# A fused three-branch token mixer on one core: attention steps moved in among the transposed products, and the gate path taken out of their evictions

## What is computed

```
h = RMSNorm(x)
(qa,ka,va,za, qb,ckv,iq,ik,iw,zb, qc,kc,vc,zc, ga,gb,gc) = split(h @ w_in)
ya = attention_A(qa, ka, va, sink, t5) * silu(za)     # 16 heads, window of 2 chunks of 64
yb = attention_B(qb, latent keys chosen by top-k 64 of an indexer) * silu(zb)
yc = attention_C(qc, kc, vc, relative bias) * silu(zc)
merged = sigmoid(ga)*(ya@w_pa) + sigmoid(gb)*(yb@w_pb) + sigmoid(gc)*(yc@w_pc)
out = RMSNorm(x + merged @ w_o)
```

## Time and profile before

| | |
|---|---|
| median of 3 runs | 973.84 us |
| the profiled execution | 973.51 us, of it 971.6 us span |
| TensorE busy | 961.6 us (99%) |
| weight loads of TensorE busy | 813.1 us (84%) |
| VectorE busy | 608.5 us (63%) |
| ScalarE busy | 473.0 us (49%) |
| GpSimd busy | 28.2 us (3%) |
| mean granted clock of TensorE | 0.997 |
| HBM | 195 GB/s over the span |

### The profile page before, as it was taken

One profiled execution on the slowest core, in us unless ns is written; L12 is line 12 of the kernel. 1 busy time (PEld: TensorE's weight loads), 2 busy tenths in 40 slices (PEclk: granted clock), 3 DMA queues, 4 the chain that ended last, 5 costly groups with the idle time before them and its releaser, 6 DMA issues.

```text
span 971.6 us, 13291 instructions
## 1 busy us (share of the span) xinstructions
PE 961.6 (99%) x5114; PEld 813.1 (84%) x5114; DVE 608.5 (63%) x1135; ACT 473.0 (49%) x786; POOL 28.2 (3%) x26
## 2 busy tenths in 40 slices
PE   9999999999999999999999999999999999999996
PEld 8788888888888888888888888888888888888885
DVE  7585755777675776586765655766655555555553
ACT  6564544555454545454453545544534443444442
POOL 0030000000000110010000000000000000000000
PEclk9999999999999999999999999999999999999998
DMA  8754755464653755564654745646555576555553
GB/s 342 274 194 130 244 200 187 151 225 162 207 205 120 253 174 180 189 207 157 222 199 139 261 157 178 227 149 216 167 193 179 191 304 221 186 184 187 174 177 126
DMA packets 54766, 190.34 MB, mean 196 GB/s; under 512 B 6192, under 2 KB 7088, under 8 KB 54064
## 3 DMA queue, kind: packets, MB, share of 16 engines
q1 hardware_dynamic: 54416, 189.23, 56.9%
q10 hardware_dynamic: 288, 0.27, 0.1%
HBM read 187.38 MB, written 2.10 MB: 195 GB/s over the span
## 4 chain that ended last, share of the span: by engine, by line
PE 94%; DVE 2%; DMA 2%; issue 1%; ACT 0%; SPq 0%; POOLq 0%; POOL 0%; DVEq 0%; ACTq 0%
PE bank L1025 23%; PE bank L1006 18%; PE bank L1008 18%; PE bank L1007 18%; PE bank L1028 12%; PE bank L981 2%; PE bank L1061 2%; PE bank L1081 2%; DMA raw<-in_w_s_dram 2%; DVE w_lo L626 1%; DVE hT L693 0%; ACT w_hi L444 0%; PE bank L1198 0%; DVE scores L686 0%; DVE denom L678 0%
## 5 line engine op out<-in xcount | busy, mean ns | idle before, releaser
L626 DVE TENSOR_TENSOR w_lo<-raw,w_hi 128x1024 fp32r<-128x1024 f32 (+2 forms) x326 | 387.2, 1211 | 172.8 <-ACT w_hi L444 171.4
L444 ACT ACTIVATE w_hi<-raw 128x1024 fp32r<-128x1024 f32 (+2 forms) x326 | 334.8, 1046 | 297.0 <-PE bank L1008 204.0
L1025 PE MATMUL bank<-hT,w_hi 128*128 128x512 f32 x976 | 306.2, 397 | 0.0
L1008 PE MATMUL bank<-w_hi,hT 128*128 128x512 f32 x568 | 221.1, 389 | 0.0
L1028 PEld LDWEIGHTS bank<-hT,w_lo 128*128 128x128 f32 x976 | 181.1, 188 | 41.1
L1006 PE MATMUL bank<-w_hi,hT 128*128 128x512 f32 x504 | 197.2, 391 | 0.0
L1007 PE MATMUL bank<-w_lo,hT 128*128 128x512 f32 x504 | 196.1, 389 | 0.0
L1028 PE MATMUL bank<-hT,w_lo 128*128 128x256 f32 x976 | 190.8, 278 | 0.0
L1025 PEld LDWEIGHTS bank<-hT,w_hi 128*128 128x128 f32 x976 | 150.6, 189 | 3.9
L1008 PEld LDWEIGHTS bank<-w_hi,hT 128*128 128x128 f32 x568 | 106.6, 188 | 22.3
L1006 PEld LDWEIGHTS bank<-w_hi,hT 128*128 128x128 f32 x504 | 94.6, 188 | 20.4 <-issue 0.2
(11 more groups left out here) (149 smaller groups left out, 559.6 us busy)
## 6 DMA issues: line engine op xcount, KB each, us to landing
raw<-in_w_s_dram SPq DMA_DIRECT2D x314, 512.0 KB, 4.4
bias_t<-in_bias_dram SPq DMA_DIRECT2D x24, 384.0 KB, 3.1
raw<-in_w_s_dram SPq DMA_DIRECT2D x6, 456.0 KB, 5.7
merged<-in_x_dram SPq DMA_DIRECT2D x2, 1024.0 KB, 10.5
raw<-in_w_s_dram SPq DMA_DIRECT2D x8, 256.0 KB, 3.1
big<-in_x_dram SPq DMA_DIRECT2D x1, 2048.0 KB, 9.8
out_dram<-big SPq DMA_DIRECT2D x8, 256.0 KB, 2.6
big<-in_x_t_dram SPq DMA_DIRECT2D x7, 256.0 KB, 5.9
```

The source lines that it names most:

```text
L444: nc.scalar.activation(halves(g)[0], raw[:, s, 0:n], ACT.Copy).then_inc(hi_ready, 1)
L626: nc.vector.tensor_tensor(low, raw[:, s, 0:n], high.bitcast(F32), ALU.subtract).then_inc(lo_ready, 1)
L1008: ins = mm(acc, xl, wh[:, e, :], start=False, stop=kt == n_kt - 1)
L1025: mm(bank[2 * (c % 2) + n][:, :], wh[:, e, n * P:(n + 1) * P], hl_t[:, kt, :, :], start=kt == 0, stop=False)
```

## The change

```diff
-CHUNKS = ([("kvc", 0, 0), ("v", 0, 0), ("v", 0, 1), ("iq", 0, 0), ("ka", 0, 0)] + quarters("q", 0) + quarters("z", 0)
+CHUNKS = ([("kvc", 0, 0), ("v", 0, 0), ("v", 0, 1), ("iq", 0, 0), ("ka", 0, 0)] + quarters("q", 0)
           + [k for u in range(4) for k in (("q", 1, u), ("uk", 0, u))]
           + [("q", 2, 0), ("uv", 0, 0), ("q", 2, 1), ("uv", 0, 1), ("q", 2, 2), ("q", 2, 3)]
-          + quarters("k", 0) + quarters("z", 1)
-          + branch(0) + quarters("z", 2) + branch(1) + branch(2) + quarters("o", 0))
+          + quarters("k", 0) + quarters("z", 0) + quarters("z", 1) + quarters("z", 2)
+          + branch(0) + branch(1) + branch(2) + quarters("o", 0))
...
 def slots():
-    yield -1, FIRST[AT["z", 0, 3]]
-    whole = [g for g in range(FIRST[AT["q", 1, 0]], END["k", 0, 3]) if KIND_OF[g] in "qk"]
-    for i in range(8):
-        yield i, whole[2 + 6 * i]
-    for b in range(2):
-        yield 8 * b + 8, FIRST[AT["z", b + 1, 0]] + 2
-        for k in range(7):
-            yield 8 * b + 9 + k, FIRST[AT["g", b, 0]] + 2 + 6 * k
+    for i in range(-1, 7):
+        yield i, FIRST[AT["q", 1, 0]] + 2 + 5 * (i + 1)
+    for i in range(7, 24):
+        yield i, FIRST[AT["k", 0, 0]] + 6 + 7 * ((i - 7) // 2) + 5 * (i % 2 == 0)
...
-        silu = sb("silu", [P, 8, SEQ])
+        silu = sb("silu", [P, 2, SEQ])
...
@@ SyncE
-                bias_at[SLOT_G[2 * (p // 2) - 3] + 5 + p % 2] = p
+                bias_at[SLOT_G[2 * (p // 2) - 3] + 6 + p % 2] = p
...
@@ ScalarE
+                    elif q >= 0:
+                        sc.wait_ge(pv_ready, q + 1)
+                        sc.wait_ge(scored, min(q + 2, NPAIR // 2))
+                        for p in (2 * q, 2 * q + 1):
+                            for t in range(NT):
+                                nc.scalar.activation(qT[p // 8][:, p % 8, P * t:P * (t + 1)],
+                                                     bank[4 + 2 * (p % 2) + t][:, SROW:CH], ACT.Copy, scale=0.25
+                                                     ).then_inc(o_ready, 1)
                 for e in range(2):
-                    p = scored_at(g - 3 - e) + e
+                    p = scored_at(g - 2 - e) + e
...
@@ VectorE
-                    elif q >= 0:
-                        ve.wait_ge(pv_ready, q + 1)
-                        ve.wait_ge(scored, min(q + 2, NPAIR // 2))
-                        for p in (2 * q, 2 * q + 1):
-                            for t in range(NT):
-                                cols = slice(P * t, P * (t + 1))
-                                nc.vector.scalar_tensor_tensor(
-                                    qT[p // 8][:, p % 8, cols], bank[4 + 2 * (p % 2) + t][:, SROW:CH], 0.25,
-                                    silu[:, p % 8, cols], ALU.mult, ALU.mult).then_inc(y_ready, 1)
                 for e in range(2):
-                    p = scored_at(g - 2 - e) + e
+                    p = scored_at(g - 1 - e) + e
...
+                        if p > 1:
+                            ve.wait_ge(o_ready, 2 * p - 2)
...
-                    p = scored_at(g - 4 - e) + e
+                    p = scored_at(g - 3 - e) + e
...
@@ VectorE, end of a z chunk (silu_chunk)
-                wait(ve, y_ready, 2 * 8 * b)
...
-                        silu[:, 2 * u + half, :], gate[:, half, 0:SEQ], 1.0, gate[:, half, SEQ:CH], ALU.add, ALU.mult)
+                        silu[:, half, :], gate[:, half, 0:SEQ], 1.0, gate[:, half, SEQ:CH], ALU.add, ALU.mult)
                 ins.then_inc(dve_evac, 1)
+                ve.wait_ge(dve_evac, dves_before(c + 1))
+                ve.wait_ge(o_ready, 4 * (4 * b + u + 1))
+                for half in range(2):
+                    m = 2 * u + half
+                    nc.vector.tensor_tensor(qT[b][:, m, :], qT[b][:, m, :], silu[:, half, :], ALU.mult
+                                            ).then_inc(y_ready, 1)
...
-            rounds = {("z", 0, 0): 0, ("z", 0, 1): 1, ("z", 0, 2): 2, ("z", 0, 3): 3, ("q", 1, 1): 4, ("q", 1, 3): 5,
-                      ("q", 2, 1): 6, ("q", 2, 3): 7}
+            rounds = {("q", b, u): 4 * b + u - 4 for b in (1, 2) for u in range(4)}
...
@@ TensorE, odd step
-                    wait(pe, y_ready, 4 * q)
+                    wait(pe, o_ready, 4 * q)
```

More of the change, by code:

```diff
@@ L282, in hybrid_trunk @@
         pv_ready = sem("pv_ready")
+        o_ready = sem("o_ready")
         y_ready = sem("y_ready")
@@ L492, in yT_split @@
             def yT_split(b, k):
-                sc.wait_ge(y_ready, 2 * (8 * b + 4 * k + 4))
+                sc.wait_ge(y_ready, 8 * b + 4 * k + 4)
+                if b > 0:
+                    sc.wait_ge(used, END["P", b - 1, 3])
                 nc.scalar.activation(y_hi[:, 4 * k:4 * k + 4, :], qT[b][:, 4 * k:4 * k + 4, :], ACT.Copy
```

## The result

| | before | changed |
|---|---|---|
| median, 7 runs each | 973.2 us (972.79 to 974.21) | 977.4 us (976.61 to 978.65) |
| profiled execution, span | 973.51, 971.6 us | 977.97, 976.2 us |

A forecast was written before the change was run, and what follows sets the result against it. TensorE, busy 99% of the span, was taken as the bound. New waits of 4.9 us less 0.3 before gave +4.6 on the profiled 973.51, so 978.1; with 0.33 for the median, 978.4 us, range 973.8 to 984.0.

The forecast's parts named there:

- The term is 0: TensorE: the 16 moved steps gain and lose nothing by their neighbours, 2.97 us per odd step in both places.
- each cycle loses 1.45 us of slack: Attention chain before even steps: deadline 2.8 us sooner, chain start only 1.35 us sooner.
- New prices: Output copies on ScalarE taken at 0.95 us; silu multiplication of two 128x256 at 0.76, plus about 0.1 for waiting.
- Steps -1 and 1: Cycles with uk chunk ends: transposes due at 12.65, second normalising done at 13.35; 0.75 us wait each, 1.5 together.
- Step 11: Cycle with z end at the third piece and two GpSimd additions: 1.7 us wait, or 0.4 if normalising is not held.
- Step 9: Cycle with k end at the second piece and two GpSimd additions: chain ends at 14.25, 0.2 us wait.
- Step 7: Cycle with k end at the first piece and two GpSimd additions: chain ends at about 14.95, 0.9 us wait.
- 15, 17 and 19: Cycles of these odd steps, without GpSimd additions: waits of 0.2, 0.05 and 0.35 us.
- The room holds: Rival: chains end 0.7 us sooner and most waits vanish; 974.8 us, or 973.8 with step 11 not held; chance 0.22.
- Collide wherever they meet: Rival: each of six GpSimd additions holds VectorE 1.8 us in the chain; 985.6 us; chance 0.10.
- Late weights: Rival: a weight piece comes 1.69 us late in each of eight z cycles; about 5 us more, 983.4; chance 0.11.

The follow-up runs named there:

- eight: Changed kernel with step pairs every eight pieces (six from odd to even, two from even to odd) and top-k rounds earlier; 972.01 us, 0.9986.
- early_rounds: Changed kernel with the eight top-k rounds moved to other pieces, out of the cycles of steps -1, 1, 3 and 5; 978.17 us, 1.0047.
- no_mask: Changed kernel without GpSimd's mask additions, so branch B attends to keys not chosen; 974.19 us, 1.0009.
- bias5: Changed kernel with a step's two bias loads one weight load earlier in SyncE's order, as before the change; 976.65 us, 1.0034.
- late_attend: Changed kernel with bias and maximum, exponentials and normalising put back one iteration later, as before the change; 1020.04 us, 1.0479.
- gap6: Changed kernel with each even step one piece later, six behind the odd one, the next odd step one piece behind; 974.83 us, 1.0014.
- mult_later: Changed kernel with a z chunk's two silu multiplications three pieces later, behind that iteration's normalising; 978.51 us, 1.0052.

## Why the prediction was right

**The sign, the size and the place were right.** Forecast 978.4 us, measured 977.4; of the difference 0.6 us is the kernel before, which this set of runs has at 973.2 and the first had at 973.84. The loss was forecast at 4.6 us and is 4.2. A part of that closeness is luck: of the eight waits, five were forecast 1.3 us too long together and three 0.9 us too short. What was right beyond the sum is the mechanism: each chain of some twenty terms ended within 0.35 us of its forecast. The end of the second normalising, in us from T0:

```
step        0     2     8    10    12    16    18    20
forecast 13.35 13.35 14.95 14.25  15.9  14.2  14.1 14.35
changed   13.2  13.2  14.6  14.5  16.0  14.1  14.2 14.15
```

The transposes were due at 14.04 where the forecast had 14.05, and at 12.9 in the steps 0 and 2 where it had 12.65.

- *"The term is 0" for the moved steps, "each cycle loses 1.45 us of slack".* The matmul counts are the same, and waits and stretch grew together. That the slack is the cause, eight shows: with six pieces in place of five ahead of each even step no wait is left. The term itself is small but not 0. The prediction measured a step only up to the first product behind it. In the kernel before, the first product behind a step is followed late, by 0.31 to 0.34 us, in both places; but among row products another six to nine then start up to 0.236 us apart, where the usual is 0.227. Behind a step among transposed products there is no such tail. Counted from the product ahead of a step over 24 products, less their usual pace, an odd step costs 3.20 us among row products and 3.16 to 3.18 among transposed ones (branches B and C), an even one 1.37 against 1.32 to 1.34. Of the 16 moved steps 14 stood among row products (8 and 16 did not), so the move gave back some 0.5 us.
- *New prices.* Four output copies took 0.79 us where I took 0.95, two multiplications 0.76 as taken. The rows (view of groups, changed kernel):

```profile
L458 ACT ACTIVATE big<-bank 128x128 f32<-128x128 f32 x32 | 6.3, 284 | 22.0 <-PE bank L1085 18.8 <-PE bank L1065 3.1
...
L784 DVE TENSOR_TENSOR big<-big,silu 128x256 f32<-128x256 f32 x16 | 6.1, 422 | 0.3
```

- *Steps -1 and 1, 0.75 us each.* They were 0.38 and 0.36, and the mis-sized term is mostly the deadline: 0.23 us of the difference. The products of the uk piece took 1.49 us (161.02 to 162.51), not 1.4, and the next product but one came 0.10 late. The chain ended 0.15 us sooner than forecast, and early_rounds, whose chain ends at the same 13.2, shows that the round isn't in it.
- *Step 11, "1.7 us, or 0.4 if the second addition does not hold the normalising".* 2.04, and no_mask 0.17. The recorded 1.7 doesn't follow from its own sum, which ends at 15.9 with the transposes due at 14.05, or 1.85; nor does 0.4, since 1.7 us less of holding leaves 0.15. The two runs settle the question that the prediction left to a page. The four L686 took 2.60 us beside the addition and 1.01 without it; one of them alone lasted 1.94. They have one input in SBUF and a scalar, and were held as the operations with two inputs are. The rule of the Trainium skill, page "SBUF — State Buffer", section "Who interferes with whom", agrees if `tensor_scalar` on SBUF runs in a two-port mode. The trace shows that it was held. For the mode it has only the pace, and the prediction's "which no row shows" overlooked it (view of groups, kernel before):

```profile
L686 DVE TENSOR_SCALAR scores<-scores,r_denom 128x128 f32<-128x128 f32 x48 | 13.5, 280 | 0.0
L686 DVE TENSOR_SCALAR scores<-scores,r_denom 128x256 f32<-128x256 f32 x32 | 11.2, 351 | 0.6
...
L799 DVE TENSOR_TENSOR merged<-merged,gate 128x512 f32<-128x512 f32 x6 | 3.9, 684 | 0.0
```

  128 more columns cost `tensor_scalar` 71 ns, 0.55 ns each. From L784 (256 columns, 422 ns) to L799 (512, 684 ns) a `tensor_tensor` pays 1.02 ns each. So `tensor_scalar` went through its columns at nearly twice the pace. That fits a mode of its own but does not show which.
- *Step 9, 0.2 us.* It was 0.52: the second addition (323.44) met a `w_lo`, which then took 2.82 us. The prediction gives only the end of this chain, 14.25, and not its terms; it was 14.5.

```profile
323.44 1.85 POOL L424 TENSOR_TENSOR bias_t<-bias_t,chosen 128x768 f32<-128x768 f32 x1 [3.02 <-DMA bias_t<-in_bias_dram]
323.56 2.82 DVE L633 TENSOR_TENSOR w_lo<-raw,w_hi 128x1024 fp32r<-128x1024 f32 x1 [0.23 <-ACT w_hi L441]
```

- *Step 7, 0.9; 15, 17 and 19, 0.6 together.* 0.62, and 0.56 together.
- *The rivals.* "The room holds" would have left 1.3 us of waits, or 0.3 with step 11 not held; there are 4.5. "Collide wherever they meet" asked for 2.2, 1.9 and 3.4 us at the steps 8, 10 and 12; they wait 0.62, 0.52 and 2.04, though no_mask shows that the additions are behind 3.0 of the 4.5 us. "Late weights": ScalarE waits less for them than before, and bias5 raised that wait by 10 us at no cost. (The price of that rival was too low by its own terms: half of 1.69 us in eight cycles is 6.8 us, not 5.)

One step of my reasoning behind the prediction failed outright, in the expectation of late_attend: an iteration of delay was reckoned at the length of what it puts in front, and cost the distance to the next gate. The same view would have told how much of the change's room its earlier iterations make.

What stays open: the last 0.5 us by which eight's stretch is under those of both other kernels. I have no row for it.

## What to carry to other kernels

When work is hidden behind a bounding engine, count for each deadline the chain of in-order operations that must be done by then, with the ends of chunks that fall between; the busy share of the helping engines (62% and 49% here, 63% and 49% before) did not show it. An operation on an in-order engine stands behind whatever waits there for the bounding engine, so a place one iteration later can cost the distance to that gate (up to 6 us in late_attend), not the length of one operation. And when one consumer's deadline is moved back, look at the next consumer on the same rotation: gap6 cured the even steps and made two odd ones wait; eight pieces for the pair cured both.

## What the runs showed of the hardware

**`tensor_scalar` with one SBUF input is held by GpSimd's addition**: 2.60 us for four beside one in the changed kernel and 2.64 in bias5, against 1.01 without. The hold works the other way too: the addition that began at 343.44, beside a `w_lo` that ran from 343.09 to 344.32, took 2.58 us where one alone took 1.85.

**A wait of some 2 us may or may not lower TensorE's clock.** In the profiles of the changed kernel and of early_rounds TensorE waits nearly the same time at step 12 and then does the same matmuls. The granted clock of the stretch from the transposes on (column PEclk), first of the changed kernel, then of early_rounds:

```profile
353.90:359.50 5.60, 5.60 (x37) 5.07 (x38) 4.25 (x5) 1.93 (x3) 0.00 (x0) 1.00 0.81 261
```

```profile
353.40:359.00 5.60, 5.56 (x27) 4.90 (x28) 4.34 (x5) 1.93 (x3) 0.00 (x0) 0.70 0.78 255
```

37 matmuls fall into those 5.6 us in one and 27 in the other, which ran partly at 1.2 GHz. At 0.70 of full speed the stretch lost about 0.30 x 5.6 = 1.7 us. Early_rounds' stretch has 1.6 us more than the changed kernel's (600.3 against 598.7), 0.2 of it longer waits, and mult_later was granted 0.70 in the same place. So a wait of 2 us costs 2 us in some executions and over 3 in others. It fits the spread of the runs, if roughly: of the 7 of the changed kernel the slowest two, 978.65 and 978.44, had a mean clock of 0.996 and 0.997 (but so had its 977.13, 0.997), and mult_later's two above 979 had 0.995 and 0.996, its two below 978 0.998 and 0.999. Of eight's and no_mask's 20 runs, which have no such wait, none was under 0.997.
